# Samples' attention in one inference step: scores and mixing in four column tiles of 32

## The reference

```python
def fox_block(qb, cq, q_pos, k, v, ck, k_pos):   # 16 heads of 64
    s = jnp.einsum('bqhd,bshd->bhqs', qb.astype(jnp.float32), k) * DH_F ** -0.5
    s = s + jnp.swapaxes(cq, 1, 2)[..., :, None] - jnp.swapaxes(ck, 1, 2)[..., None, :]
    s = jnp.where(k_pos[None, :] <= q_pos[:, None], s, -jnp.inf)
    p = jax.nn.softmax(s, axis=-1)
    return jnp.einsum('bhqs,bshd->bqhd', p, v).astype(qb.dtype)
...
        k_all = jnp.concatenate([ck.astype(f32), k.astype(f32)], axis=1)   # 512 old + 16 new
        v_all = jnp.concatenate([cv.astype(f32), v.astype(f32)], axis=1)
        c_all = jnp.cumsum(jnp.concatenate([clf.astype(f32), log_ff], axis=1), axis=1)
        y_f = fox_block(q, c_all[:, P:], P + jnp.arange(T), k_all, v_all, c_all, jnp.arange(P + T))
```

## Time and profile before

| | |
|---|---|
| median of three runs | 5133.01 us |
| lowest, highest | 5125.77, 5140.24 us |
| the profiled execution: its span, from first to last instruction | 5137.4 us |
| TensorE busy in it | 4489.3 us, 87% |
| VectorE, ScalarE, GpSimd busy | 3085.4, 953.6, 1252.6 us |
| mean DMA rate | 288 GB/s |
| samples' scores, first to last start of L1249 | 574.3 to 859.9 us |

### The profile page before, as it was taken

How to read it: one execution, slowest core, us unless ns; L and a number is a source line. 1 busy time by engine, 2 the same in 40 slices (tenths; PEclk the granted TensorE clock), 3 DMA queues, 4 the chain that set the end, 5 groups by cost and what they waited for, 6 DMA issues and landing times. The chain is left out here.

```text
span 5137.4 us, 47634 instructions
## 1 busy us (share of the span) xinstructions
PE 4489.3 (87%) x16494; PEld 2746.5 (53%) x16494; DVE 3085.4 (60%) x6265; ACT 953.6 (19%) x1784; POOL 1252.6 (24%) x970
## 2 busy tenths in 40 slices
PE   8996698885999996888887898836999999999989
PEld 5555454553555554666664565635555455454534
DVE  1003322067766665888884366787777777777742
ACT  1113111110011101555542112112000000000023
POOL 0000022001444442333330000000544444444410
PEclk9998788997999998777877999979999999999999
DMA  4433452963999998888776777445999999999951
GB/s 165 144 127 100 158 195 92 357 231 144 422 381 388 394 378 291 314 300 306 297 289 249 287 288 260 172 164 193 416 418 419 416 418 415 414 414 413 414 208 57
DMA packets 338721, 1477.65 MB, mean 288 GB/s; under 512 B 38146, under 2 KB 153650, under 8 KB 217938
## 3 DMA queue, kind: packets, MB, share of 16 engines
q0 software_dynamic: 119872, 824.76, 39.9%
q1 hardware_dynamic: 218642, 650.30, 34.2%
HBM read 1369.00 MB, written 115.38 MB: 289 GB/s over the span
## 5 line engine op out<-in xcount | busy, mean ns | idle before, releaser
L2287 POOL DMA_INDIRECT ex_uv<-in_uv,idx x768 | 1161.5, 1512 | 1936.8 <-DVE ex_acc L2344 1688.4
L2328 DVE CUSTOM_DVE_ANT_0 ex_uv<-ex_uv,ex_xp 128x1024 f32<-128x1024 f32 x768 | 913.8, 1221 | 313.4 <-DMA ex_uv<-in_uv,idx 274.7
L2344 DVE SCALAR_TENSOR_TENSOR ex_acc<-ex_uv,ex_wt,ex_acc 128x1024 f32<-128x1024 f32 x768 | 943.1, 1281 | 10.0 <-DVE C L880 3.2
L384 PE MATMUL proj_psum_acc<-proj_w,aT_later 128*128 128x385 f32 x2304 | 749.0, 487 | 63.2 <-DMA proj_w<-in_w_in 63.2
L2634 PE MATMUL exp_psum_dn<-exp_dn_big,exp_dn_gg 128*128 128x512 f32 x1536 | 689.6, 599 | 24.1 <-DVE exp_dn_gg L2556 24.1
L2625 PE MATMUL exp_psum_dn<-exp_dn_xT,exp_dn_big 128*128 128x384 f32 x2048 | 683.5, 487 | 14.1 <-DMA exp_dn_big<-in_ud 14.1
L384 PEld LDWEIGHTS proj_psum_acc<-proj_w,aT_later 128*128 128x128 f32 x2304 | 437.1, 190 | 374.7 <-DMA proj_w<-in_w_in 63.4
L2625 PEld LDWEIGHTS exp_psum_dn<-exp_dn_xT,exp_dn_big 128*128 128x128 f32 x2048 | 390.2, 191 | 313.9 <-issue 61.9
L2634 PEld LDWEIGHTS exp_psum_dn<-exp_dn_big,exp_dn_gg 128*128 128x128 f32 x1536 | 293.3, 192 | 375.8 <-issue 347.4
L296 PE MATMUL proj_psum_acc<-proj_w,aT 128*128 128x385 f32 x1152 | 378.1, 489 | 5.1 <-DMA proj_w<-in_w_in 3.3
L1956 PE MATMUL rt_psum_b<-rt_w,rt_yT 128*128 128x512 f32 x576 | 270.4, 633 | 50.3 <-ACT rt_yT L2022 42.4
(11 more groups left out here) (374 smaller groups left out, 4448.4 us busy)
## 6 DMA issues: line engine op xcount, KB each, us to landing
proj_w<-in_w_in SPq DMA_DIRECT2D x48, 1540.0 KB
rt_w<-in_w_q SPq DMA_DIRECT2D x36, 2048.0 KB, 8.0
exp_dn_big<-in_ud SPq DMA_DIRECT2D x128, 512.0 KB
exp_dn_big<-in_vd SPq DMA_DIRECT2D x128, 512.0 KB, 8.0
scratch_z<-proj_zs SPq DMA_DIRECT2D x216, 192.5 KB, 1.9
rt_w<-in_w_br_m SPq DMA_DIRECT2D x18, 2048.0 KB, 9.8
rt_w<-in_w_br_f SPq DMA_DIRECT2D x18, 2048.0 KB
rt_w<-in_w_out SPq DMA_DIRECT2D x18, 2048.0 KB, 8.1
```

Of the source, the lines that this page charges most:

```text
L384: mm = pe.matmul(acc[j % SLOTS][:, 0:CW], aT[:, k, t * P:(t + 1) * P], w[:, u % U, k, :], start=(k == 0), stop=(k == KD - 1))
L2287: pool.indirect_dma_start(self.uv[:, slot, :], None, self.uv_tab, bass.IndirectOffsetOnAxis(ap=self.idx[:, at:at + 1], axis=0)).then_inc(s ...
L2328: dve.tensor_tensor_reduce(self.uv[:, slot, 0:D], self.uv[:, slot, 0:D], self.xp[:], 1.0, 0.0, ALU.mult, ALU.add, self.dot[:, g % 2, j:j + ...
L2344: dve.scalar_tensor_tensor(out=self.acc[:, j % 2, :], in0=self.uv[:, slot, D:2 * D], scalar=self.wt[:, g % 2, j:j + 1], in1=self.acc[:, j ...
```

## The change

The two kinds of large matmuls now work by pairs of heads, each pair in its own 32 columns of the array, so in its own 32 output partitions.

- `qd` keeps only the 32 columns of the pair: 128 by 32 for each p. It is cleared as 512 columns instead of 2048, and `diag4`, which addressed the diagonal, is gone.
- Scores: the four matmuls over the old keys write 32 rows each, each with start=True; the four over the new keys follow at once, and then come both decay rows (128 output rows, added to what is there) and the mask.
- Mixing: for each block of keys four matmuls, the pair's 32 columns of `probT` with the pair's 128 value columns; the same for the new values. The output is 128 by 128: partition 16h holds head h in half h mod 2.
- VectorE multiplies 128 by 128, and the DMAs take their pieces from the halves.

```diff
--- before.py
+++ after.py
@@ -1159,6 +1159,7 @@
     S = PAST + DSEQ
     ST = PAST // P
     STEPS = 2 * NSEQ
+    PAIR = 2 * DSEQ
 
     def __init__(self, nc, K, st, z, T):
         self.K, self.T, self.z = K, T, z
@@ -1166,10 +1167,10 @@
         self.kc, self.vc = st.sb("skc", [P, 2, KD, PAST]), st.sb("svc", [P, 2, self.ST, W_F])
         self.q, self.k = self.vc[:, 1, 0, :], self.vc[:, 1, 1, :]
         self.vn, self.ck = st.sb("svn", [DSEQ, 2, W_F]), st.sb("sck", [H_F, 2, self.S])
-        self.kn, self.qd = st.sb("skn", [P, 2, KD, DSEQ]), st.sb("sqd", [P, 2, 2, 4, P])
+        self.kn, self.qd = st.sb("skn", [P, 2, KD, DSEQ]), st.sb("sqd", [P, 2, 2, 4, 2 * DSEQ])
         self.prob, self.probT = st.sb("sprob", [P, 2, self.S]), st.sb("sprobT", [P, 5 * P])
         self.nmax, self.total, self.inv = (st.sb(n, [P, 2]) for n in ("snmax", "stotal", "sinv"))
-        self.y = st.sb("sy", [P, 2, 512])
+        self.y = st.sb("sy", [P, 2, 2 * DF])
         self.s_ps, self.t_ps, self.y_ps = st.ps("ss", [P, 1024]), st.ps("st", [P, 512]), st.ps("sy", [P, 512])
         (self.zeroed, self.qk_in, self.t_full, self.t_free, self.placed, self.scored, self.maxed, self.expd,
          self.inverted, self.mixed, self.y_ready) = st.sems(
@@ -1218,7 +1219,7 @@
         for h in range(8):
             c = W_M + (8 * f + h) * DF
             pool.dma_start(self.T["ycat"][n * DSEQ:(n + 1) * DSEQ, c:c + DF],
-                           self.y[h * DSEQ:(h + 1) * DSEQ, f, h * DF:(h + 1) * DF]).then_inc(self.y_out[f], 16)
+                           self.y[h * DSEQ:(h + 1) * DSEQ, f, h % 2 * DF:(h % 2 + 1) * DF]).then_inc(self.y_out[f], 16)
 
     def pool_last(self, pool):
         for f in range(2):
@@ -1246,10 +1247,12 @@
         sel = self.K["headsel"][:, f].rearrange("p h q -> p (h q)")
         old, new = self.s_ps[:, 0:PAST], self.s_ps[:, PAST:self.S]
         for p in range(4):
-            pe.matmul(old, self.qd[:, b, f, p, :], self.kc[:, b, 4 * f + p, :], start=(p == 0), stop=False)
+            at = slice(self.PAIR * p, self.PAIR * (p + 1))
+            pe.matmul(old[at], self.qd[:, b, f, p, :], self.kc[:, b, 4 * f + p, :], start=True, stop=False)
+        for p in range(4):
+            at = slice(self.PAIR * p, self.PAIR * (p + 1))
+            pe.matmul(new[at], self.qd[:, b, f, p, :], self.kn[:, b, 4 * f + p, :], start=True, stop=False)
         pe.matmul(old, sel, self.ck[:, b, 0:PAST], start=False, stop=True)
-        for p in range(4):
-            pe.matmul(new, self.qd[:, b, f, p, :], self.kn[:, b, 4 * f + p, :], start=(p == 0), stop=False)
         pe.matmul(new, sel, self.ck[:, b, PAST:self.S], start=False, stop=False)
         pe.matmul(new, self.K["ident"][:], self.K["masknew"][:], start=False, stop=True).then_inc(self.scored, 1)
 
@@ -1271,11 +1274,17 @@
             pe.wait_ge(self.vc_in[b], (n // 2 + 1) * 32)
         if s >= 1:
             pe.wait_ge(self.y_ready, s)
+        W = 2 * DF
         for c in range(self.ST):
-            pe.matmul(self.y_ps[:], self.probT[:, c * P:(c + 1) * P], self.vc[:, b, c, f * 512:(f + 1) * 512],
-                      start=(c == 0), stop=False)
-        pe.matmul(self.y_ps[:], self.probT[0:DSEQ, self.ST * P:(self.ST + 1) * P], self.vn[:, b, f * 512:(f + 1) * 512],
-                  start=False, stop=True).then_inc(self.mixed, 1)
+            for p in range(4):
+                at, cols = slice(self.PAIR * p, self.PAIR * (p + 1)), slice(f * 512 + p * W, f * 512 + (p + 1) * W)
+                pe.matmul(self.y_ps[at, 0:W], self.probT[:, c * P + at.start:c * P + at.stop], self.vc[:, b, c, cols],
+                          start=(c == 0), stop=False)
+        for p in range(4):
+            at, cols = slice(self.PAIR * p, self.PAIR * (p + 1)), slice(f * 512 + p * W, f * 512 + (p + 1) * W)
+            mm = pe.matmul(self.y_ps[at, 0:W], self.probT[0:DSEQ, self.ST * P + at.start:self.ST * P + at.stop],
+                           self.vn[:, b, cols], start=False, stop=True)
+        mm.then_inc(self.mixed, 1)
 
     def dve_first(self, dve):
         dve.memset(self.qd[:], 0.0).then_inc(self.zeroed, 1)
@@ -1290,9 +1299,8 @@
         t = slice(n * DSEQ, (n + 1) * DSEQ)
         for f in range(2):
             for e in range(2):
-                flat = self.qd[e * DF:(e + 1) * DF, b, f, :, :].rearrange("p c m -> p (c m)")
-                dve.tensor_copy(diag4(flat, e * DSEQ), self.qT[e * DF:(e + 1) * DF, 4 * f:4 * f + 4, t]
-                                ).then_inc(self.placed, 1)
+                dve.tensor_copy(self.qd[e * DF:(e + 1) * DF, b, f, :, e * DSEQ:(e + 1) * DSEQ],
+                                self.qT[e * DF:(e + 1) * DF, 4 * f:4 * f + 4, t]).then_inc(self.placed, 1)
         dve.tensor_copy(self.kn[:, b], self.kT[:, :, t]).then_inc(self.placed, 1)
 
     def dve_max(self, dve, s):
@@ -1310,7 +1318,8 @@
         dve.wait_ge(self.mixed, s + 1)
         if n >= 1:
             dve.wait_ge(self.y_out[f], n * 8 * 16)
-        dve.tensor_scalar(self.y[:, f, :], self.y_ps[:], self.inv[:, f:f + 1], None, ALU.mult).then_inc(self.y_ready, 1)
+        dve.tensor_scalar(self.y[:, f, :], self.y_ps[:, 0:2 * DF], self.inv[:, f:f + 1], None, ALU.mult
+                          ).then_inc(self.y_ready, 1)
 
     def act_first(self, act):
         for g in range(4):
@@ -1681,13 +1690,6 @@
                    ap=[v.ap[0], [NSEQ * P, 2], [P + DSEQ, NSEQ], [1, DSEQ]])
 
 
-def diag4(flat, first):
-
-    step = P + 2 * DSEQ
-    v = flat[:, first:first + 3 * step + DSEQ]
-    return bass.AP(tensor=v.tensor, offset=v.offset, ap=[v.ap[0], [step, 4], [1, DSEQ]])
-
-
 def stage_sample(nc, K, z, gates, T):
 
     with Stage(nc, "smp") as st:
```

## The result

The changed kernel takes 5021.26 us (median of 4 runs, 5019.13 to 5022.75), the kernel before, run beside it, 5130.88 (4 runs, 5125.77 to 5140.24): ratio 0.9782, 95% interval 0.9768 to 0.9796. It is faster by 109.6 us where 45.9 were forecast, and lies outside the range of 5053 to 5140. The profiled execution's span is 5020.9 us, 116.5 less than before's.

A forecast was written before the change was run, and what follows sets the result against it. TensorE's own instruction stream was taken to bound the samples' stage. Savings of 15 x 1.65 us (scores), 16 x 1.25 (mixing) and 1.1 (first step) sum to 45.9, off the median 5133.0 giving 5087; range 5053 to 5140.

The forecast's parts named there:

- The step that failed: Samples' stage, matmul order: only neighbouring passes of different tiles overlap, so old-key scores take 2.27 us, old-value mixing 2.35.
- rival A: Scores and mixing: all four tiles run at once, saving 89 us in all, to 5044; chance 0.12.
- the small terms: New keys and new values in each step: 0.60 us for new keys, 0.70 plus 0.09 on each side for new values.
- rival C: Samples' stage: lower clock granted more often with part of the array at work; 35 us slower, 5168; chance 0.09.
- A pass never starts ahead of one in front of it: TensorE's pass order, read from the trace before; basis for old-key scores of 2.27 us.
- the decay row and the mask: End of each step's scores: old keys' decay row 0.97 us, new keys' 0.31, mask 0.24.
- the price of a change of mode: Entering the column tiles before scores and before mixing: 0.10 us each.
- no new wait for ScalarE, GpSimd or cache loads: Samples' stage: softmax, stores and cache loads charged nothing; wait before mixing stays at 0.3 us, DMA share about 52%.
- the first step: Start of the samples' stage: shorter clearing and first scores' saving together keep only 1.1 us, because z's loads land later.
- Rival B: Scores and mixing: tiles run one behind another; 7 us faster, 5126, or 16 slower, 5149, with loads exposed; chance 0.25.

The follow-up runs named there:

- the three orders of the mixing: Changed kernel with the mixing's 16 old-value matmuls reordered: one tile after another, two tiles alternating, or runs of two per tile; 5042.57, 5028.32 and 5022.37 us.
- tile by tile: Changed kernel with the mixing's old-value matmuls reordered, all four key blocks of one tile before the next tile; 5042.57 us.

## Why the prediction was wrong

- **The step that failed**: "The second pass of tile 0 has to wait for the first, in the same quarter; everything behind it waits too". Only the first half is true. Passes for other quarters go past, as long as no more than three wait in one quarter, which is the reading that fits the three orders of the mixing (2.39, 1.47 and 1.05 us). So all four tiles run at once, rival A, which had 0.12. Old keys take 0.89 us instead of the forecast's 2.27 (A: 0.86), old values 1.01 instead of 2.35 (A: 0.96). In the table that is 25.5 + 22.7 = 48.2 us of the 66 by which the stage was missed.
- **In A too the small terms were too dear.** New keys cost 0.16 us and not 0.60: their eight passes overlap as well, and the small weight load isn't paid one by one. New values cost 0.35, not 0.70 + 2 x 0.09. Together 14.8 us. I had overlapped the large matmuls and counted the small ones one after another.
- **The clock, which rival C had falling.** Its mean over the stage fell a little, from 0.88 to 0.85, and not below C's 0.73. Behind the scores it rose: 6.7 us that neither the sum nor a rival had, which with the small terms took the gain beyond A's 89 us. The mean of the whole stage hid this, while in five of the eight steps with only pairs and transposes there, it went from between 0.56 and 0.63 in the 3.9 us behind the scores to 1.00. My first windows were as long as the stage, or held only its start.
- **The reliance on habit.** "A pass never starts ahead of one in front of it" was read from rows in which no two quarters were at work, and across quarters it doesn't hold: tile by tile, tile 1's first pass starts at 605.639, ahead of tile 0's sixth at 605.742. What stays in order is the handing out, and within a quarter the starts. The Trainium skill (TensorE: Matmul & The Clock Gate, Part 3: Packing small matmuls) gives 2.38 times for three column tiles and says that matmuls start and end in program order. This case goes beyond the first, 0.89 us for 3.53 with four tiles, and its starts don't agree with the second. The page's estimate of about 4 ns a tile is 7 ns in this trace, where a tile has two passes.
- **Right**: TensorE was the bound of the stage and what came off it came off the end (111.8 us of the stage, 109.6 of the time); the decay row and the mask (0.96, 0.22, 0.24 against 0.97, 0.31, 0.24); the price of a change of mode; no new wait for ScalarE, GpSimd or cache loads, although the DMA share went to 71% instead of 52%; and the first step, which keeps 1.0 us where 1.1 was forecast, because z comes when it comes (4.6 us of waiting, and with the long clearing 3.0).
- **Rival B** is out: with the tiles one behind another old values would have taken 3.52 us. Passes of one tile start 0.109 us apart when it runs alone; 32 of them in 1.01 us must overlap.

## What to carry to other kernels

Where a matmul's output uses only its own rows or columns of a wider tile, cut it into column tiles of 32 and send the tiles in turn. Here four float32 streams then cost what one did (0.89 us instead of 3.53), runs of four passes in one quarter were free and runs of eight were not (1.05 and 2.39 us), and the small matmuls gained as well. Before pricing what stands around it, look at the granted clock in stretches of a few microseconds, here right behind runs of short matmuls; a mean over the stage hides it. And when the only open question is whether two things overlap, both answers deserve a real chance: the gain here was a matter of 46 or about 110 us.

## What the hardware showed that I had not expected

- Four 512-column passes in four column quarters start within 20 ns (7 ns apart, 3.3 ns for each pass handed out); mixing goes in rounds of four, 0.109 us apart, which is the time of one 128-column pass.
- A quarter seems to hold three passes behind the running one; the next that doesn't fit stops the stream for all quarters (tile by tile, 2.39 us instead of 1.01).
- 32-column weight loads run one round ahead, in every quarter at once: eight in 0.16 us, four of them under running passes.
- A change from full width to column tiles costs 0.09 us (0.310 instead of 0.217 us to the next start).
- At a mean granted clock of 0.57 the same matmuls took 3.94 us instead of 2.34 at 1.00, with TensorE busy without a gap in both. What stood in front of the fall was a run of short passes at full width, not idle time.
